# Sums of squares of heads in four row groups, page and state transfers in twos, one more empty step, state rows two steps later

## What is computed

```python
def l2_normalize(x):
    xf = x.astype(jnp.float32)
    return xf * lax.rsqrt(jnp.sum(jnp.square(xf), axis=-1, keepdims=True) + EPS)

def rms_norm(x, g):
    xf = x.astype(jnp.float32)
    y = xf * lax.rsqrt(jnp.mean(jnp.square(xf), axis=-1, keepdims=True) + EPS)
    return (y * g.astype(jnp.float32)).astype(x.dtype)

def gdn_recurrent(q, k, v, g, beta, s0):     # the sample tokens
    ...
        s = jnp.exp(g_t)[..., None, None] * s
        u = b_t[..., None] * (v_t - jnp.einsum('bhk,bhkv->bhv', k_t, s))
        s = s + jnp.einsum('bhk,bhv->bhkv', k_t, u)

def page_block(phys):                        # for each of the 128 pages
    kn, kr, v = mla_keys(cache_l[phys], w_uk, w_uv, k_norm_nope)
    return partial_softmax(mla_scores(qn, qr, kn, kr), v)
```

## Time and profile before

| | us |
|---|---|
| median of three executions | 1406.71 |
| lowest, highest | 1405.67, 1407.85 |
| the profiled execution, its own time | 1409.61 |
| its span, first to last instruction | 1407.8 |

### The profile page before, as it was taken

The page is one execution under the profiler, slowest core; times in us unless marked ns, Lnnn a source line. Parts: engine busy times, 40 slices in busy tenths (PEclk is TensorE's granted clock), DMA queues, the critical chain, the costliest instruction groups (busy, mean ns, idle before and its releaser), DMA issues.

```text
span 1407.8 us, 29929 instructions
## 1 busy us (share of the span) xinstructions
PE 1383.4 (98%) x9380; PEld 1169.1 (83%) x9380; DVE 990.4 (70%) x3646; ACT 855.0 (61%) x2780; POOL 294.1 (21%) x339
## 2 busy tenths in 40 slices
PE   9999999999999999999999999999999999999998
PEld 7877887887787877778777887778778999999998
DVE  5767667778776877867777778768665567777543
ACT  5445688687666786666866667866773453444332
POOL 3012222223332222322222322322331000000000
PEclk9999999999999999999999999999999999999999
DMA  9442326744545653356454474444564575555551
GB/s 282 126 119 58 82 47 147 168 108 96 95 97 145 141 133 77 79 145 155 100 114 86 102 160 94 102 98 90 118 166 158 172 239 163 167 180 180 180 181 59
DMA packets 285449, 183.33 MB, mean 130 GB/s; under 512 B 184608, under 2 KB 231232, under 8 KB 285288
## 3 DMA queue, kind: packets, MB, share of 16 engines
q1 hardware_dynamic: 284978, 181.16, 50.6%
q10 hardware_dynamic: 318, 0.33, 0.1%
HBM read 137.56 MB, written 6.80 MB: 103 GB/s over the span
## 4 chain that ended last, share of the span: by engine, by line
PE 81%; DVE 6%; SPq 4%; ACT 4%; DMA 3%; issue 2%; POOL 0%; DVEq 0%; ACTq 0%
PE ps L2108 14%; PE ps L2110 13%; PE ps L2109 13%; PE ps L2503 6%; PE ps L2504 6%; PE ps L2505 6%; DMA turned<-planes 2%; PE ps L2130 2%; PE ps L2451 2%; PE ps L2452 2%; PE ps L2453 2%; PE ps L2183 2%; PE ps L2184 1%; PE ps L2185 1%; SPq L538 1%
## 5 line engine op out<-in xcount | busy, mean ns | idle before, releaser
L2108 PE MATMUL ps<-ukh,cTh 128*128 128x512 f32 x1024 | 417.8, 408 | 8.6 <-DVE sparts L1326 7.8
L937 ACT ACTIVATE ksq<-ps 128x128 f32<-128x128 f32 x1024 | 266.8, 275 | 226.9 <-PE ps L2110 226.3
L2110 PE MATMUL ps<-ukh,cTl 128*128 128x512 f32 x1024 | 401.4, 392 | 0.0
L2109 PE MATMUL ps<-ukl,cTh 128*128 128x512 f32 x1024 | 401.2, 392 | 0.0
L1326 DVE CUSTOM_DVE_ANT_0 prod<-ps,qb 128x128 f32<-128x128 f32 x1024 | 234.1, 284 | 25.4 <-ACT ksq L937 21.5
L2108 PEld LDWEIGHTS ps<-ukh,cTh 128*128 128x128 f32 x1024 | 193.9, 189 | 65.5 <-issue 27.4
L2110 PEld LDWEIGHTS ps<-ukh,cTl 128*128 128x128 f32 x1024 | 193.0, 188 | 42.8
L2109 PEld LDWEIGHTS ps<-ukl,cTh 128*128 128x128 f32 x1024 | 193.7, 189 | 34.3
L789 POOL TENSOR_TENSOR rk<-kss,mhalf 128x8 f32<-128x8 f32 x128 | 219.1, 1712 | 10.6
L937 ACT ACTIVATION_READ_ACCUMULATOR ksq<-ps 128x1 f32 x1024 | 211.3, 206 | 0.0
L924 ACT ACTIVATE cTr<-turned 128x1024 uint16<-128x1024 uint16 x126 | 174.4, 1384 | 6.4 <-DMA turned<-planes 6.3
(11 more groups left out here) (498 smaller groups left out, 2662.8 us busy)
## 6 DMA issues: line engine op xcount, KB each, us to landing
clat<-cache_mla SPq DMA_DIRECT2D x128, 256.0 KB, 2.6
wraw<-w_in SPq DMA_DIRECT2D x16, 1024.0 KB, 5.4
wraw<-w_up SPq DMA_DIRECT2D x16, 1024.0 KB, 5.4
wraw<-w_down SPq DMA_DIRECT2D x16, 1024.0 KB, 5.0
braw<-w_in SPq DMA_DIRECT2D x24, 512.0 KB, 4.1
crope<-cache_mla SPq DMA_DIRECT2D x128, 32.0 KB, 2.4
qb<-scratch SPq DMA_DIRECT2D x16, 256.0 KB, 3.5
sst<-state_gdn SPq DMA_DIRECT2D x32, 128.0 KB, 4.0
```

What stands on the lines that cost most here:

```text
L937: i = nc.scalar.activation(ksq[m % 3], ps[:, k % 3, P * h:P * h + P], ACT.Square, accum_out=kss[:, n // 4 % 2, n % 4, h0 + h:h0 + h + 1]). ...
L2108: mm(out, cTh[:, n % 2, c], ukh[:, c, cols], start=c == 0, stop=False)
L2109: mm(out, cTh[:, n % 2, c], ukl[:, c, cols], start=False, stop=False)
L2110: i = mm(out, cTl[:, n % 2, c], ukh[:, c, cols], start=False, stop=c == 3)
```

## The change

It does four things. (1) `l2r` and `osr`: head c is summed into rows 32c of PSUM with the same `window(0, 32)`, each matmul for itself, instead of accumulating into one block; the copies take 128 and 64 partitions, and `compact` reads partition 32c. (2) The four pages of i % 8 == 3 become two there and two in i % 8 == 5; the eight state loads of k = 2 go in twos to k = 4, 6, 8, 10; the eight state writes of k = 43 go in twos to k = 43, k = 44 (after the convolution rows) and p = 0 and 3 of the next pair. (3) `STEPS` gets a second None ahead of k = 17, so a pair has 51 slots, pairs start in slots 35, 86, 137 and 188, and the tail, the last scaling and `z_load` come up to four slots later (`z_load` in slot 245). (4) The convolution rows are turned on PE and copied by ACT at k = 3 instead of k = 1.

```diff
@@ -135,7 +135,7 @@
 ROOT, ROOT_OUT, ROOT_BACK = 47, 48, 49
-STEPS = list(range(14)) + [None, 14, 15, 16, ROOT, ROOT_OUT, ROOT_BACK, None] + list(range(17, 45))
+STEPS = list(range(14)) + [None, 14, 15, 16, ROOT, ROOT_OUT, ROOT_BACK, None, None] + list(range(17, 45))
 B_START, B_SLOTS = F_END + 6, len(STEPS)
@@ -312,7 +312,7 @@
         assert e <= C_NEG.stop * 4
-        lr, e = place("lr", [4, T], F32, taken["krT"][0])
+        lr, e = place("lr", [P, T], F32, taken["krT"][0])
         lc, e = place("lc", [88, 4, 12], F32, e)
@@ -575,7 +575,7 @@
                 for c in range(n_):
-                    sp.dma_start(lc[22 * c:22 * c + 22, 0, :], lr[c:c + 1, :].rearrange("c (a b) -> c a b", b=12)).then_inc(S("compacted"), 16)
+                    sp.dma_start(lc[22 * c:22 * c + 22, 0, :], lr[32 * c:32 * c + 1, :].rearrange("c (a b) -> c a b", b=12)).then_inc(S("compacted"), 16)
 
@@ -585,7 +585,16 @@
 
+            def states_out(b, s0):
+                sp.wait_ge(S("a_read"), a_count(f"out3_{b}"))
+                for s_ in range(s0, s0 + 2):
+                    sp.dma_start(O["gdn_sample"][0, s_, 2 * b:2 * b + 2].rearrange("h k v -> k h v"), sst[:, s_]).then_inc(S("gdn_out"), 16)
+
             def tail_loads(b, p):
+                if p == 0:
+                    states_out(b, 4)
+                if p == 3:
+                    states_out(b, 6)
                 if p == 1:
@@ -600,10 +609,10 @@
                     pair_weights(6 * b + k // 2 + 3)
-                if k == 2:
+                if k in (4, 6, 8, 10):
                     if b >= 1:
                         sp.wait_ge(S("gdn_out"), 16 * 9 * b)
-                    for s_ in range(NS):
+                    for s_ in range(k - 4, k - 2):
                         sp.dma_start(sst[:, s_], I["state_gdn"][0, s_, 2 * b:2 * b + 2].rearrange("h k v -> k h v")).then_inc(S("sst_landed"), 16)
@@ -614,11 +623,11 @@
                     compact(f"osr_{b}", 2)
-                    sp.wait_ge(S("a_read"), a_count(f"out3_{b}"))
-                    for s_ in range(NS):
-                        sp.dma_start(O["gdn_sample"][0, s_, 2 * b:2 * b + 2].rearrange("h k v -> k h v"), sst[:, s_]).then_inc(S("gdn_out"), 16)
-                if k == 44 and b + 1 < HP:
-                    pair_rows_in(b + 1)
+                    states_out(b, 0)
+                if k == 44:
+                    if b + 1 < HP:
+                        pair_rows_in(b + 1)
+                    states_out(b, 2)
 
@@ -666,7 +675,10 @@
                     sp.wait_ge(S("pv_used"), i // 8 - 1)
-                    for m in range(n, n + 4):
+                    for m in range(n, n + 2):
+                        page(m % RING, m)
+                if i % 8 == 5 and i >= 16 and n + 1 < NT:
+                    for m in range(n + 1, n + 3):
                         page(m % RING, m)
@@ -1003,7 +1015,7 @@
                     pair_high(6 * b + k // 2 + 1)
-                if k == 1:
+                if k == 3:
                     nc.scalar.activation(csT[:].rearrange("p c n -> p (c n)"), rows_out(f"cs_{b}")[:, 0:144], ACT.Copy).then_inc(S("b_read"), 1)
@@ -1563,7 +1575,7 @@
                 if k == 14:
-                    V.tensor_scalar(lr[:], bank("l2r")[0:4, 0:T], 1.0, EPS, ALU.mult, ALU.add).then_inc(S("a_read"), 1)
+                    V.tensor_scalar(lr[:], bank("l2r")[:, 0:T], 1.0, EPS, ALU.mult, ALU.add).then_inc(S("a_read"), 1)
                 if k == ROOT:
@@ -1711,7 +1723,7 @@
                 if k == 42:
-                    V.tensor_scalar(lr[0:2], bank("osr")[0:2, 0:T], 1.0 / P, EPS, ALU.mult, ALU.add).then_inc(S("a_read"), 1)
+                    V.tensor_scalar(lr[0:64], bank("osr")[0:64, 0:T], 1.0 / P, EPS, ALU.mult, ALU.add).then_inc(S("a_read"), 1)
 
@@ -2204,7 +2216,7 @@
                     for c in range(4):
-                        i = mm(p_[0:32, 0:T], window(c, 32), lsq[:, c, :], start=c == 0, stop=c == 3)
+                        i = mm(p_[32 * c:32 * c + 32, 0:T], window(0, 32), lsq[:, c, :], start=True, stop=True)
                     a_done(i)
@@ -2325,7 +2337,7 @@
                     for hh in range(2):
-                        i = mm(p_[0:32, 0:T], window(hh, 32), osq[:, hh, :], start=hh == 0, stop=hh == 1)
+                        i = mm(p_[32 * hh:32 * hh + 32, 0:T], window(0, 32), osq[:, hh, :], start=True, stop=True)
                     a_done(i)
```

## The result

The changed kernel took 1398.31 us (median of four, 1397.55 to 1398.78), the kernel before 1407.28 beside it (1405.67 to 1409.74): ratio 0.9934, 95% interval 0.9917 to 0.9951, 9.0 us faster. The time lies in the range of 8 in 10 (1384 to 1400), but outside the forecast's own band (1384 to 1394) and its bounds (1386 to 1395), 8.8 us above the predicted 1389.5: about half of the 17.2 us came (9.0). The profiled execution of after took 1398.12 us with a span of 1396.3.

A forecast was written before the change was run, and what follows sets the result against it. PE, busy 98% of the span, was taken as the bound. Terms 7.0 + 5.7 + 5.0 + 2.0 + 0.5 - 3.0 = 17.2 us off the 1406.7 median gave 1389.5, with an 8-in-10 range of 1384 to 1400.

The forecast's parts named there:

- both old stalls: PE's 2.64 us wait for convolution rows in pair 1, and its wait for DVE from 712.06 to 715.64.
- Row groups, 7.0 us: In `l2r` and `osr`, matmuls in separate row groups overlap, saving PE 1.32 and 0.42 us in each of four pairs.
- Rows at k = 3, 5.7 us: In pair 1, PE's 2.64 us wait for convolution rows and the half clock after go, nothing late next: 5.7 us.
- pair 2, 5.0 us: PE's stall on DVE, itself waiting for `hrows`, goes whole: 3.35 us, plus 1.7 of half clock, together 5.0.
- rival 2: SP's queue: spacing does nothing, bytes in flight cause lateness; only PE's 7.0 us gained, 1399.7; chance 0.11 shared with the third.
- The empty step itself costs nothing: In each pair, the added step holds no PE work, so it costs nothing while PE is the bound.
- End of the loop, -2.0 us: With `z_load` in slot 245 behind the last pages, 2.0 of 3.1 us of PE idle time go.
- The cover for the weights themselves: After `z_load`, four slots less leave 10.4 us for a 1 MB transfer that lands in 5.4, or 10.8 if held up.
- Charge of 3.0 for new stalls: Pairs meet page slots in another phase, so some `turn` comes late elsewhere: bounded by zero and 6 us, charged 3.
- The first: Rival: shifted phases make a new meeting of burst, root and `turn` that replaces one stall; 1397, chance 0.20.
- The third: Rival: row groups in the sums don't overlap, so their 7.0 us is lost; 1396.5, chance 0.11 shared with rival 2.
- The fourth: Rival: SP's wait at k = 4 holds the `turn` in pairs 1 to 3, 5.7 us each; 1416.8, chance 0.05.

## Why the prediction was right and wrong, step by step

The direction was right, and its cause: both old stalls are gone, and the groups work as worked out. That the time fell into the range is in part luck: the range was wide enough for the rivals, and the wait for `bwl` was in no term of the sum, while the one new stall cost 7.5 us where a stall was bounded at 6 and charged at 3.

- *Row groups, 7.0 us: right in size.* Timeline of PE after, as the earlier trace rows:

```profile
300.28 0.63 PE L2219 MATMUL ps<-lsq,consts_sb 128*32 128x264 f32 x8
300.84 0.51 PE L2120 MATMUL ps<-ukh,cTh 128*128 128x512 f32 x1
...
415.68 0.64 PE L2340 MATMUL ps<-osq,consts_sb 128*32 128x264 f32 x4
416.25 0.50 PE L2120 MATMUL ps<-ukh,cTh 128*128 128x512 f32 x1
```

  0.56 and 0.57 us from start to start, the 0.56 that was worked out; the four pairs differ by 0.03. That all of it arrives held for 6.0 us in the pairs of the full change and for 4.5 by itself; the rest came back as waits of PE.
- *Rows at k = 3, 5.7 us, and pair 2, 5.0 us: the gain came, but was credited to single edits.* Both stalls and both half clocks are gone. But the pages in twos remove both half clocks and nearly all of the stalls alone, and the rows at k = 3 alone hand 1.3 of their 5.7 us to the next late `turn`. The step "with nothing late next" was wrong for the edit alone, and right only beside the spaced queue. (The "13 us before the `turn`" under rival 2 are 12.0 by the earlier trace rows; nothing else rests on it.)
- *"The empty step itself costs nothing": wrong.* It asked whether the step holds work of PE, and left out that 51 is odd. Pairs 1 and 3 changed sides in the two slots of a page, and DVE's work for them came too late: 3.2 us. What it was credited with, the room for `hrows`, was worth next to nothing once the pages went in twos (3.1 us between the pairs' stages with and without it, of which `bwl` is 3.0). This is most of the 3.8 us missing in the pairs: 18.2 - 3.2 = 15.0, and 14.4 came.
- *End of the loop, -2.0 us: wrong in sign.* The prediction had seen that the `turn` of slot 246 travels with the 2 MB, as that of slot 242 did, and took the cost to be the same. Before, slot 241 held the 2 MB alone. After, slot 245 held the last two pages, the 2 MB and then the `turn`: 9.14 us to land, 4.67 us of stall and 2.8 of clock. It counted the pages no longer behind the 2 MB as a gain and didn't write out what the queue held in slot 245. The cover for the weights themselves held: the first megabyte landed 6.05 us after its issue at 1017.46, and ACT first read at 1029.64, 12.2 us after it, of which the stall made 4.67.
- *Charge of 3.0 for new stalls: too small.* They came to 3.2 us for `bwl` and 7.5 for the stall in front of slot 249. With that in place of the charge, 20.2 - 10.7 = 9.5, where 9.0 was measured.
- *Rivals.* The first (one stall takes the place of an old one; 1397) is what happened, at 1398.3, and at the place that it named, the end of the loop; the 3.2 us of `bwl` were not in it. The second (spacing does nothing, 1399.7) hit the time for no right reason: spacing alone gives 12.7 us. The rule of the Trainium skill behind it (DMA: Bandwidth & Descriptors, Issuing engines are not separate DMA queues), that the time to initiate is usually small beside the transfer, isn't borne out by this queue: a state write took 0.545 us of issue for 2.0 us to land, and eight of them one after the other 4.36. Bytes in flight do count beside the 2 MB. The third (groups don't overlap) is refuted by the 0.56. The fourth (slower, SP held at k = 4) isn't seen: among SP's waits between 236 and 1060 us none stands at the state loads.
- *The signs to look for.* "A new wait of PE for DVE over 2.5 us, followed by half clock" was named as the mark of rival 1, and is what the trace shows. Of the marks of a right forecast, 0.56 us for `l2r`, no idle time at the convolution rows and no wait for `hrows` are met; that no `turn` goes out over 4 us after its planes is not (the one at 428.03 went out 5.0 us after them, without a stall), nor is the loop without half clock.

## What to carry to other kernels

Where PE is the bound and one queue feeds it, write out what the queue holds in each slot, before and after: a change of period moves every coincidence, and the collision that it makes may be worth more than the one that it removes. Issue large transfers behind the small ones that somebody waits for, see what then stands behind them (the pages in the kernel with all pairs in even slots), and break bursts before moving their users. An empty step is free only if the number of slots keeps the side (odd or even) on which the other engines' work falls.

## What the runs showed of the hardware

- The order of two transfers in one queue was worth microseconds: of the 126 transposing transfers of the changed kernel half landed in 3.03 to 3.18 us, and the one right behind 2 MB of weights in 9.14, at 313 GB/s in that stretch. Issued right ahead of them it landed in 3.65, and the next, 3.1 us behind the first megabyte, in 6.0. A late landing alone cost nothing: with the empty step at the pair's end one took 7.97 us, and PE's waits for DVE between 1020 and 1050 us came to 0.4.
- In these runs the stalls of PE in the loop that took 2.63 to 4.67 us had 3.41 or 6.83 us at half clock behind them, and those of 1.98, 2.10 and 2.29 us had none. Stalls of the same size had either length: 3.34 us was followed by 3.41 and 3.33 us by 6.83; 4.67 us by 6.83 in the changed kernel and by 3.41 in the one without groups. So the price of one such stall is known only to within 1.7 us.
- In the changed kernel two matmuls in two row groups took 0.57 us and four in four groups 0.56 to 0.59; accumulated into one block they took 0.98 to 1.01 and 1.87 to 1.90.
